# Gated rows, forgetting queries and keys of the first block turned on VectorE with a block exchange through device memory

## What is computed

```python
h = _rmsnorm(x, g_mix)
(gq, gk, gv, gg, ga1, fq, fk, fv, ff, mq, bg) = split(h @ w_in)
o_gla = _rmsnorm(_gla(gq, gk, gv, log_a), g_gla_out)        # 4 heads of 128
y_gla = _merge(o_gla) * silu(gg)                            # 256 x 512
o_fox = _fox(_rmsnorm(fq, g_fox_q), _rmsnorm(fk, g_fox_k), fv, log_f)
#   softmax(q_t.k_s/sqrt(128) + sum_{s<j<=t} log f_j, causal), 4 heads of 128
o_mem = _cross(_rmsnorm(mq, ..), _rmsnorm(mk, ..), mv)
gates = sigmoid(bg + b_gate)
merged = sum_i gates_i * (y_i @ w_branch_i)
x = x + merged @ w_out          # then an FFN, then the second block
```

## Time and profile before

| | us |
|---|---|
| median of 3 runs | 1100.97 |
| lowest and highest | 1100.49, 1100.97 |
| the profiled execution's own time | 1100.77 |
| its span, first to last instruction | 1098.8 |
| busy: TensorE, weight loads | 1090.5, 906.3 |
| busy: VectorE, ScalarE, GpSimd | 843.9, 663.9, 194.9 |

### The profile page before, as it was taken

How to read it: one execution, slowest core, us unless ns; L and a number is a source line. 1 busy time by engine, 2 the same in 40 slices (tenths; PEclk the granted TensorE clock), 3 DMA queues, 4 the chain that set the end, 5 groups by cost and what they waited for, 6 DMA issues and landing times.

```text
span 1098.8 us, 12971 instructions
## 1 busy us (share of the span) xinstructions
PE 1090.5 (99%) x5095; PEld 906.3 (82%) x5095; DVE 843.9 (77%) x956; ACT 663.9 (60%) x811; POOL 194.9 (18%) x135
## 2 busy tenths in 40 slices
PE   9999999999999999999999999999999999999997
PEld 7788888888888888888888888888888888888886
DVE  5785668776569998678538569999677976799974
ACT  6646566654767765654588366576455645655651
POOL 1434700000343420000013000004306000000430
PEclk9999999999999999999999999999999999999999
DMA  9745444545555489655534546459855344544970
GB/s 350 250 171 191 132 172 154 215 173 191 177 194 206 168 207 317 228 215 190 193 115 170 194 173 245 175 171 259 296 191 215 106 163 171 203 180 160 251 240 38
DMA packets 31800, 214.60 MB, mean 195 GB/s; under 512 B 3768, under 2 KB 3936, under 8 KB 6912
## 3 DMA queue, kind: packets, MB, share of 16 engines
q1 hardware_dynamic: 28320, 195.61, 48.9%
q0 software_dynamic: 3424, 18.23, 8.0%
HBM read 212.77 MB, written 1.05 MB: 195 GB/s over the span
## 4 chain that ended last, share of the span: by engine, by line
PE 93%; DVE 4%; ACT 1%; issue 1%; DMA 0%; SPq 0%; DVEq 0%; ACTq 0%
PE ps L789 77%; PE ps L1318 3%; PE aux L862 3%; PE ps L1266 2%; PE aux L1266 2%; PE ps L1320 1%; DVE Wl L2044 1%; PE ps L905 1%; PE aux L1111 1%; PE aux L1355 1%; PE aux L1096 1%; ACT Wh L1484 1%; PE ps L982 0%; PE aux L1342 0%; DMA mrows<-in_mem 0%
## 5 line engine op out<-in xcount | busy, mean ns | idle before, releaser
L789 PE MATMUL ps<-Wh,xT 128*128 128x512 f32 x1792 | 559.9, 391 | 0.0
L2044 DVE TENSOR_TENSOR Wl<-raw,Wh 128x2048 fp32r<-128x2048 f32 (+1 forms) x188 | 437.4, 2336 | 126.6 <-ACT Wh L1484 125.0
L1484 ACT ACTIVATE Wh<-raw 128x2048 fp32r<-128x2048 f32 (+1 forms) x192 | 366.0, 1914 | 169.7 <-PE ps L789 155.8
L789 PEld LDWEIGHTS ps<-Wh,xT 128*128 128x128 f32 x1792 | 336.4, 188 | 69.8 <-issue 0.3
L789 PE MATMUL ps<-Wl,xT 128*128 128x512 f32 x896 | 348.6, 389 | 0.0
L789 PEld LDWEIGHTS ps<-Wl,xT 128*128 128x128 f32 x896 | 168.3, 188 | 34.1
L2652 DVE STREAM_TRANSPOSE htmp<-held 32x512 f32<-32x512 f32 x128 | 89.9, 703 | 2.5
L789 PE MATMUL ps<-Wh,hTh 128*128 128x512 f32 x192 | 74.8, 390 | 0.0
L789 PE MATMUL ps<-Wh,hTl 128*128 128x512 f32 x192 | 74.7, 389 | 0.0
L789 PE MATMUL ps<-Wl,hTh 128*128 128x512 f32 x192 | 74.7, 389 | 0.0
L693 POOL DMA_DIRECT2D raw<-in_wstream x12 | 10.7, 890 | 249.6 <-DVE Wl L2044 249.6
(11 more groups left out here) (419 smaller groups left out, 1537.8 us busy)
## 6 DMA issues: line engine op xcount, KB each, us to landing
raw<-in_wstream SPq DMA_DIRECT2D x182, 1024.0 KB, 4.8
raw<-in_wstream POOLq DMA_DIRECT2D x12, 1024.0 KB, 8.6
grow<-in_post_gains POOLq DMA_DIRECT2D x4, 512.0 KB, 5.9
grow<-in_b_gate POOLq DMA_DIRECT2D x6, 256.0 KB, 3.5
mrows<-in_mem SPq DMA_DIRECT2D x2, 512.0 KB, 5.5
raw<-in_wstream SPq DMA_DIRECT2D x2, 512.0 KB, 6.7
x<-in_x SPq DMA_DIRECT2D x1, 1024.0 KB, 14.7
out<-x SPq DMA_DIRECT2D x4, 256.0 KB, 2.0
```

What stands on the lines that cost most here:

```text
L789: mm = nc.tensor.matmul(ps[2 * pair + t][:, :], a[:, kt, t * P:(t + 1) * P], w[:, slot, j, :], start=(first and j == 0 and q == 0), stop=( ...
L1484: nc.scalar.activation(split_view(Wh, g), weight_view(raw, g), ACT.Copy).then_inc(hi_ready, 1)
L2044: nc.vector.tensor_tensor(split_view(Wl, g), weight_view(raw, g), split_view(Wh, g).bitcast(F32), ALU.subtract).then_inc(lo_ready, 1)
```

## The change

TensorE's 24 transposes of FQ, FK and GG and their six PSUM banks go. In their place VectorE transposes each array with one instruction over all 128 partitions, which turns every 32x32 square in place (`turn_head_rows`). The squares then have to change partitions: SP writes them to device memory in four transfers of 128 KB, one per group of 32 partitions (`blocks_out`), in pieces of 1 KB, and reads them back in one of 512 KB (`blocks_in`). SP does this between its weight loads: the first write after the load of granule 21, the others after those of granules 23, 25 and 26. VectorE's transposes stand after the head sums of go (GG), after the head sums of fk (FQ), and after unit fv (FK). The read-outs now take SBUF in place of PSUM and wait for the transfers: FQ two instructions of 128x512 on ScalarE, FK two on VectorE, the low part of y_gla eight of 128x128 in place of four of 128x256. TensorE waits for a count of finished pieces (`fox_rows`) before the scores and before branch_gla0.

```diff
--- before.py
+++ after.py
@@ -218,9 +218,6 @@
     use("msc", [0, 1, 2, 3])
     use("mpT", [0, 1, 2, 3])
     use("moT", [0, 1, 2, 3])
-    use("fqT", [0, 1])
-    use("fkT", [2, 3])
-    use("gyT", [0, 1])
     use("fsc", [0, 1, 2, 3])
     use("fpT", [0, 1, 2, 3])
     use("foT", [0, 1, 2, 3])
@@ -395,6 +392,11 @@
         mqT = at("mqT", [P, 4, TOK], R + 52)
         mkT = at("mkT", [P, 4, TOK], R + 56)
         fpT = at("fpT", [P, 4, 2, TOK], R + 52)
+        blocks = {"go": at("blocks_go", [P, 4, 8, 32], R + 16), "fq": at("blocks_fq", [P, 4, 8, 32], R + 20),
+                  "fk": at("blocks_fk", [P, 4, 8, 32], R + 16)}
+        moved = {"go": at("moved_go", [P, 4, 8, 32], R + 24), "fq": at("moved_fq", [P, 4, 8, 32], R + 52),
+                 "fk": at("moved_fk", [P, 4, 8, 32], R + 56)}
+        line = {n: nc.dram_tensor(f"line_{n}", (4, 32, 4, 256), F32, kind="Internal").ap() for n in moved}
         fqT = at("fqT", [P, 4, TOK], R + 60)
         fkT = at("fkT", [P, 4, TOK], R + 64)
         mpT = at("mpT", [P, 4, 2, TOK], R + 60)
@@ -560,6 +562,21 @@
             return ins.then_inc(aux_free[AUX[(name, b)][0]], 1)
 
 
+        def moved_heads(name, t):
+            return moved[name][:, :, 4 * t:4 * t + 4, :].rearrange("p q h j -> p h q j")
+
+        def heads_at(dst, t):
+            return dst[:, :, t * P:(t + 1) * P].rearrange("p h (q j) -> p h q j", j=32)
+
+        def moved_tokens(name, h):
+            return moved[name][:, :, h::4, :].rearrange("p q t j -> p t q j")
+
+        def in_rows(v):
+            return v.rearrange("p (q j) -> p q j", j=32)
+
+        def tokens(dst, h):
+            return dst[:, h, :].rearrange("p (t q j) -> p t q j", q=4, j=32)
+
         @block.sync
         def _(sp):
             sp.dma_start(gains[:, :], gpack).then_inc(sem("gains_in"), 16)
@@ -573,7 +590,35 @@
             sp.dma_start(x[:, :, :], x_rows).then_inc(sem("x_in"), 16)
             sp.dma_start(cst[:, P:], cpack[:, P:]).then_inc(sem("cst_in"), 16)
             sp.dma_start(raw[:, 3, :, :], wstream[3]).then_inc(landed[3], 16)
+            def blocks_out(name):
+
+                sp.wait_ge(sem("blocks_turned"), list(line).index(name) + 1)
+                for q in range(4):
+                    sp.dma_start(line[name][:, :, q, :].rearrange("c i e -> i c e"),
+                                 blocks[name][32 * q:32 * q + 32, :, :, :].rearrange("p c b j -> p c (b j)"))\
+                        .then_inc(sem("line_out"), 16)
+
+            def blocks_in(name):
+
+                n = list(line).index(name)
+                sp.wait_ge(sem("line_out"), 64 * n + 64)
+                if n:
+                    sp.wait_ge(sem("line_in"), 16 * n)
+                sp.dma_start(moved[name][:, :, :, :].rearrange("p q b j -> p q (b j)"),
+                             line[name].rearrange("c i q e -> (c i) q e")).then_inc(sem("line_in"), 16)
+
             for g in range(RING, NP):
+                if g == P0["fk"] + 8:
+                    blocks_out("go")
+                elif g == P0["fk"] + 10:
+                    sp.wait_ge(sem("blocks_turned"), 2)
+                    blocks_in("go")
+                    blocks_out("fq")
+                elif g == P0["fk"] + 12:
+                    blocks_in("fq")
+                    blocks_out("fk")
+                elif g == P0["fk"] + 13:
+                    blocks_in("fk")
                 if not ADDED[g]:
                     sp.wait_ge(lo_ready, g + 1 - RING)
                     sp.dma_start(raw[:, g % RING, :, :], wstream[SRC[g]]).then_inc(landed[g % RING], 16)
@@ -1127,23 +1172,10 @@
             for h in range(4):
                 wait_read(pe, "mpT", h)
                 attend("moT", h, lambda ks: MV[:, ks, h * HD:(h + 1) * HD], mpT)
-            pe.wait_ge(sem("head_unit"), HEAD_NORMS["fq"])
-            for b in range(2):
-                turn_rows("fqT", FQ, b)
-            pe.wait_ge(sem("head_unit"), HEAD_NORMS["fk"])
-            for b in range(2):
-                turn_rows("fkT", FK, b)
-
-            def turn_gla():
-                pe.wait_ge(sem("head_unit"), HEAD_NORMS["go"])
-                for b in range(2):
-                    turn_rows("gyT", GG, b)
-
-            product("gate_gla0", (xTh, xTl), before={1: turn_gla})
-
-
-            wait_operand("fqT", range(2))
-            wait_operand("fkT", range(2))
+            product("gate_gla0", (xTh, xTl))
+
+
+            pe.wait_ge(sem("fox_rows"), 4)
             for h in range(4):
                 o = open_aux("fsc", h)
                 nc.tensor.matmul(o[:, 0:P], fqT[:, h, 0:P], fkT[:, h, 0:P], start=True, stop=True)
@@ -1159,7 +1191,7 @@
             for h in range(4):
                 wait_read(pe, "fpT", h)
                 attend("foT", h, lambda ks: FV[:, ks, h * HD:(h + 1) * HD], fpT, causal=True)
-            wait_operand("gyT", range(2))
+            pe.wait_ge(sem("fox_rows"), 12)
             product("branch_gla0", yT["gla"])
             wait_operand("foT", range(4))
             product("branch_fox0", yT["fox"])
@@ -1696,9 +1728,9 @@
 
             def fq_turned():
                 act.wait_ge(sem("q_gains"), 2)
-                for b in range(2):
-                    o = wait_aux(act, "fqT", b)
-                    free(nc.scalar.activation(fqT[:, 2 * b:2 * b + 2, :], o[:, :], ACT.Copy, scale=S("gfq_s")), "fqT", b)
+                act.wait_ge(sem("line_in"), 32)
+                for t in range(2):
+                    nc.scalar.activation(heads_at(fqT, t), moved_heads("fq", t), ACT.Copy, scale=S("gfq_s")).then_inc(sem("fox_rows"), 1)
 
             def mem_probs():
                 for h in (0, 2):
@@ -1707,8 +1739,10 @@
             unit("gate_mem0", mem_probs, mem_high, gate_log("mem", 0), fq_turned)
 
             def gla_high():
-                for b in range(2):
-                    high("gyT", b, yT["gla"][0], (2 * b, 2 * b + 1), "g_gla")
+                act.wait_ge(sem("line_out"), 192)
+                for kt in range(4):
+                    nc.scalar.activation(tokens(yT["gla"][0], kt), moved_tokens("go", kt), ACT.Copy, scale=gcol("g_gla", kt))\
+                        .then_inc(sem("gyT_hi"), 1)
                 gate_sigmoid("mem", 0)
                 gate_log("gla", 0)()
 
@@ -2246,6 +2280,15 @@
                     nc.vector.memset(S("ffa"), 0.0).then_inc(sem("gla_step"), 1)
             unit("fq")
             head_sums("go")
+
+            def turn_head_rows(key, rows):
+
+                dve.wait_ge(sem("head_unit"), HEAD_NORMS[key])
+                nc.vector.transpose(blocks[key][:, :, :, :].rearrange("p c b j -> p b c j"),
+                                    rows[:, :, :].rearrange("p t (h c j) -> p (t h) c j", c=4, j=32))\
+                    .then_inc(sem("blocks_turned"), 1)
+
+            turn_head_rows("go", GG)
             head_sums("fq")
             unit("fk")
             for h in range(4):
@@ -2265,6 +2308,7 @@
                 normed("m", h, prob, lambda a, b: S("ms_rec", 2 * h + a, 2 * h + b),
                        lambda a, b: S("ms_sum", 2 * h + a, 2 * h + b), (TOK, TOK))
             head_sums("fk")
+            turn_head_rows("fq", FQ)
             unit("fv")
 
             def gate_rows(b, n):
@@ -2312,19 +2356,28 @@
                     low("moT", h, yT["mem"][1], yT["mem"][0], (h,))
 
             def fk_turned():
-                for b in range(2):
-                    turned("fkT", b, fkT[:, 2 * b:2 * b + 2, :], gcol("g_fk"))
+                dve.wait_ge(sem("line_in"), 48)
+                for t in range(2):
+                    nc.vector.tensor_scalar(heads_at(fkT, t), moved_heads("fk", t), gcol("g_fk"), None, ALU.mult)\
+                        .then_inc(sem("fox_rows"), 1)
 
             def mem_probs():
                 for h in (1, 3):
                     turned("mpT", h, mpT[:, h, :, :])
                 gate_rows("mem", 0)()
 
+            dve.wait_ge(sem("line_out"), 64)
+            turn_head_rows("fk", FK)
             unit("gate_mem0", mem_probs, mem_low, lambda: gate_lsig("mem", 0, 0), lambda: gate_lsig("mem", 0, 1), fk_turned)
 
             def gla_low():
-                for b in range(2):
-                    low("gyT", b, yT["gla"][1], yT["gla"][0], (2 * b, 2 * b + 1), "g_gla")
+                for kt in range(4):
+                    dve.wait_ge(sem("gyT_hi"), kt + 1)
+                    for t in range(2):
+                        at0 = slice(t * P, (t + 1) * P)
+                        nc.vector.scalar_tensor_tensor(out=in_rows(yT["gla"][1][:, kt, at0]), in0=moved["go"][:, :, 4 * t + kt, :],
+                                                       scalar=gcol("g_gla", kt), in1=in_rows(yT["gla"][0][:, kt, at0]).bitcast(F32),
+                                                       op0=ALU.mult, op1=ALU.subtract).then_inc(sem("fox_rows"), 1)
                 gate_rows("gla", 0)()
 
             def fox_scores():
```

## The result

The median after the change is 1102.53 us (1101.3 to 1104.34, 22 runs), against 1100.74 us before (1100.49 to 1101.12, 22 runs): ratio 1.0017, 95% interval 1.001 to 1.0023. That lies inside the 0.2% (2.2 us) within which the prediction counts two times as the same, though the sign of the difference is clear: slower by 1.8 us. The profiled execution took 1102.9 us, with a span of 1100.9, 2.1 above that of before.

A forecast was written before the change was run, and what follows sets the result against it. TensorE is busy 1090.5 of 1098.8 us, but VectorE's chain was taken to bound the stretch before about 172 us. Chain +0.1 and late keys +1.2 on 1100.77 gave 1102.1 us, range 1100.5 to 1105.2.

The forecast's parts named there:

- the price of the keys: VectorE's wait for FK before the fkT copies: FK back at about 151.0 us, delaying the split by 1.2 us.
- that of the low part: Gated rows on VectorE: eight instructions taking 1.8 to 2.2 us against 1.65; +0.2 taken, bounds 0 and +0.6.
- rival (d): TensorE's stand from 168.7 to about 171.7 us lets its clock fall: 2.2 us more, 1104.3; chance 0.12.
- TensorE gains 2.6 us and loses them in front of the probabilities: Before the probability transposes: TensorE arrives 2.6 us earlier, at 168.7, and waits 2.6 us longer for VectorE's normalisation.
- The VectorE transposes: Three transposes on VectorE, of GG, FQ and FK: 1.24 us each, covered by idle time, cost 0.
- one for one after 151.21 - 1.40 = 149.8: At VectorE's wait for FK: lateness costs nothing up to 149.8 us, then delays the split equally, 1.2 us.
- ScalarE's fqT pair: Two copies on ScalarE from 148.11 us, now out of SBUF: 1.26 us, no change taken, between -0.2 and +0.2.
- The signs named: Expected in the profile: TensorE waiting 3 to 4 us from 168.7, about 2 us DMA wait before fkT, 1.2 us transposes.
- low part and rounding: VectorE's chain: +0.2 for the gated rows' eight instructions, -0.1 for ScalarE's earlier rounding; together +0.1 us.

The follow-up runs named there:

- the filler: The changed kernel with twelve matmuls, results thrown away, on TensorE directly before the probability transposes: 1101.56 us, ratio 1.0009.
- order changed: The changed kernel with the loads of granules 24 and 25 issued after the whole exchange instead of in its midst: 1102.44 us, ratio 1.0015.
- keys only: The changed kernel with the gated rows turned by TensorE as before, only forgetting queries and keys exchanged: 1100.92 us, ratio 1.0001.
- six turns: The kernel before with one transpose in place of four into each of six PSUM banks, six instead of 24: 1100.57 us, ratio 0.9999.
- gated rows only: The changed kernel with its low-part instructions moved into VectorE's two idle times, and queries and keys turned by TensorE again: 1099.56 us, ratio 0.9989.
- pieces of 4 KB: The changed kernel with the same bytes written to device memory in pieces of 4 KB instead of 1 KB: 1102.22 us, ratio 1.0013.

## Why the prediction was right, and where its terms were off

The time was forecast as 1102.1 (1100.5 to 1105.2) with 0.65 for no difference beyond 0.2%; it is 1102.53, inside that bound. The mechanism held: TensorE's gain is absorbed, and VectorE's chain ends later. That the sum came so close is in part luck: the price of the keys was 0.7 us too high, that of the low part 0.3 too low, and a rival with a chance of 0.12, the clock, filled the rest. Without the fall, with the filler in the stand, the kernel takes 1101.56.

- **TensorE gains 2.6 us and loses them in front of the probabilities.** Right: it arrives at 168.67, forecast 168.7, and stands 2.68 us, a little less than the 3 to 4 named among the signs. Taking most of the transposes out of the kernel before won nothing either. That nothing in this stretch is gained by TensorE's own savings could be read from the chain without a matmul from 151 to 172 us.
- **The VectorE transposes.** 1.24 us forecast, 1.24 and 1.25 measured, over all 128 partitions, at no cost to the path. The one of FK came at 136.60 rather than 135.5. The profile names the blocks of FQ as its releaser and the program has it wait for those of GG, but these had left by 119, and in the run without the exchange of GG, which has no such wait, it came at 136.59, released by GpSimd. What was late is GpSimd: its scaling of FK ran from 134.13 instead of 133.10, because its 128x8 step before (L637) took 3.35 us instead of 2.21. That step took 3.34 us in two more kernels that have VectorE's transpose of FQ ahead of its two splits (order changed, keys only) and 2.21 or 2.22 in three without it (before, six turns, gated rows only). The prediction took GpSimd's times over unchanged from the trace of before. The cover was large enough all the same: the mpT copies ran from 139.94, and TensorE didn't wait for them.
- **The keys.** FK was forecast back at about 151.0 and came at 150.86. The Trainium skill's figures in "DMA: Bandwidth & Descriptors", the section on the anatomy of one DMA, had given an estimated 144; the trace doesn't agree. That section's fit is for transfers that GpSimd issues, and it counts no queue; with the loads behind the exchange the keys still came at 147.1. The price, 1.2 us, was too high: the keys' lateness cost 0.5. **The step that failed** is "one for one after 151.21 - 1.40 = 149.8": it took 1.40 us for the fkT pair. Two copies out of PSUM took 741 ns each; out of SBUF they take 482, so from the start of the pair to the start of the split it is 0.80 us. Without the keys the split would have started at 151.18, when ScalarE's rounding lets it, which makes the deadline 150.38; the keys were 0.48 late. ScalarE's fqT pair took 1.33 us where 1.26 was assumed, inside the bounds of 0.2.
- **The low part.** Eight instructions at 0.22 to 0.28 us were forecast, +0.2 taken from bounds of 0 and +0.6; they start 0.26 apart and the group ends 0.53 later. The saving of an SBUF input, which was counted, isn't there for instructions this short: the 128x128 of L2388, which reads PSUM, also lasts 0.34, and the next instruction starts 0.26 behind it. The term was inside its bounds and near the upper end.
- **The clock, rival (d).** This was named, priced at 2.2 us for nine matmuls at the lower level and given 0.12. It happened in the profiled run, and filling the stand took 1.0 us off the median. The price was twice what was found: the level was low for about six matmuls of branch_mem0 and part of the transposes, not for nine. The chance was too low, and the reason stood in the prediction itself: it forecast a stand of 3 to 4 us in one piece while no row of the trace had one. The Trainium skill, "TensorE: Matmul & The Clock Gate", Part 1, says that an idle TensorE is throttled and has to earn its clock back; the trace now agrees (0.50 from 172.8 to 176.2 us, behind a stand of 2.68).
- **What would show it.** The signs named came true, up to the length of the stand: the groups of L862 on FQ, FK and GG gone, the stand at 168.7, 2.07 us of DMA wait before fkT, three transposes of 1.2 us, and, as the sign of (d), a clock under 1 after 170 us.

In terms of the sum: forecast +0.1 (low part and rounding) and +1.2 (keys), with the clock at 0; found, in the profiled run, +0.5 low part, +0.5 keys, -0.2 for a shorter pair of splits, +1.1 clock, and 0.2 ahead of branch_mem0 that is not told apart.

Open: why the kernel after spreads over 3 us where that of before spreads over 0.6. Part of it is the clock. Of its 22 executions three have a mean clock of 1.0 (1101.3, 1101.92 and 1102.06 us), and the two with 0.996 are the two slowest (1104.15 and 1104.34). In the two variants with the same kind of stand (order, and pieces of 4 KB) the groups don't overlap: 1101.01, 1101.2 and 1101.32 us at 1.0, and 1102.01 to 1102.91 for the nineteen at 0.997 or 0.998. Nor does every fall cost the same: in the three traces the low level lasts 3.4 us each time, from 172.8, 171.6 and 171.1 on, and branch_mem0 takes 6.63, 6.25 and 5.91 us, where it takes 5.56 before the change, at 1.00. But the kernel after also has runs of 1101.56 to 1102.0 us at 0.998, so the clock isn't all of it. What decides whether and when the clock falls in an execution, no run tells.

## What to carry to other kernels

Before taking work from the busiest engine, look in the chain for who led to its next meeting with another engine, and then for the meeting after that one: here the first lay at 171 us and the second at 187. A saving that turns into a stand of two to three microseconds can cost more than nothing, because the clock may fall with it. What an operation *occupies* (two PSUM banks) can decide whether the time that it saves ever comes through, but only once the next edit makes use of it.

## What the runs showed of the hardware that was not expected

- In all three kernels profiled with a stand of TensorE of 2.2 to 2.7 us, the granted clock went to 0.50 for 3.4 us, in one of them before the stand was over and in two during the twelve transposes spread over 2.9 us that follow it. Stands of 0.2 and 0.6 us ahead of transposes spread over 2.5 us, stands of 1.2, 1.4 and 1.7 us ahead of matmuls and scores, and no stand left it at 1.00 in the profiled executions.
- On VectorE a copy of 128x512 with a gain took 482 ns out of SBUF and 741 out of PSUM. On ScalarE the same change of source made the pair longer, 1.33 against 1.26 us. In both the pattern of the access changed too, to pieces of 32 columns. The low part's 128x128 instructions took 343 ns each, starting 0.26 us apart.
- GpSimd's 128x8 step behind VectorE's sums of FK took 3.34 to 3.35 us in three kernels whose VectorE has the FQ transpose ahead of its two splits, and 2.21 to 2.22 in three without it.
- 512 KB leaving in four transfers took 2.0 us of all 16 DMA engines, in pieces of 1 KB and of 4 KB alike.
- The three transfers that brought 512 KB back took 3.6, 6.1 and 6.7 us from issue to landing, and the four transfers of FQ and of FK that left took medians of 5.8 and 5.2 us, beside three loads of 1 MB in the same queue; those of GG, with nothing else in the queue, took 2.3.
